# Products of 512 columns that nobody reads in TensorE's waits between an MLP and a state-space block, and one scaling moved behind the second half's addition at the end

## The chip, the cores and the metric

The kernel runs on one core of one Trainium2 chip. The metric is the device time of one execution in microseconds. The kernel before was timed three times: 1705.33, 1705.75 and 1705.82 us, median 1705.75 us.

## The reference

Two transformer-like blocks act in turn on x, 512 tokens by 1024 features, all in float32. Cut to what matters here:

```python
# first block, its end
u2 = rmsnorm(h, norm_mlp_pre)
h = h + rmsnorm(square(relu(u2 @ w_up)) @ w_down, norm_mlp_post)
# second block, its beginning
hn = rms_norm(h, norm_mix_w) * (1.0 + scale) + shift      # scale, shift: from c by adaln
proj = hn @ w_in                                           # convolution, state-space heads, gates
...
# second block, its end
x = x + gate * ((silu(g) * up) @ w_ffn_down)
return rms_norm(x, final_norm_w)
```

So between the MLP and the state-space block stand two norms in a row: that of the MLP's result, and that of the new h. At the end stands one more norm, over the 1024 features of each token.

## The kernel before, in words

Everything is held transposed: 128 partitions by 512 tokens, in 8 chunks of features (`KC = 8`). A weight panel (128 x 2048) comes by DMA from SyncE's queue (`w_raw`, two slots). ScalarE rounds it to `w_hi` (lines 1195 to 1199), GpSimd writes the rest to `w_lo` in four pieces (`low_parts`, line 449). TensorE makes each output tile of 128 x 512 from three products per chunk: high weights by high operand, high weights by low operand, low weights by high operand. Tiles are numbered through the program; tile t goes to the PSUM bank `gemm_bank[t % 4]`. A semaphore `bank_free[b]` counts how often bank b was given back.

The order on each engine is written out by hand, as one program per engine, and the engines wait for each other's semaphores.

**Between MLP and state-space block.** The last tile of the MLP is tile 119, in bank 3; the first tiles of the next block are 120 (`T_DT`, panel 56), 121 and 122 (panel 57), then 123 in bank 3 again. For each token three sums over the features are needed: of the squares of y, of the squares of y times its gain, and of y times gain times h. Seven of eight chunks are added up on VectorE beforehand. TensorE turns these into sums per token by products with a column of ones (`sums_of_parts`, three groups of four; `sums_of_last`, one group of four for `cross`, and one for the last chunk's squares; a float32 product shows as two passes in the profile, so each group is eight records). Then ScalarE takes the root (line 1371), VectorE the reciprocal (line 1711), and TensorE spreads it over the partitions (`spread(3)`, line 562). VectorE scales y (`added_part`, line 2008), GpSimd adds it to h (line 465; on its queue behind the `w_lo` of panel 57), and VectorE scales the new h (`new_operand`, line 2013) by a second spread row, whose root and reciprocal come from a chain of five small steps (`new_step`). ScalarE adds the shift (line 1379), and TensorE begins `first_three` (line 831). In the waits TensorE runs transposes of the identity that nobody reads (`keep_busy`, line 746): 3 ahead of `spread(3)`, 5 behind it, 7 ahead of `first_three`.

VectorE gives bank 3 back (`bank_free[3]`) after it has added tile 119 to y (line 1959); the same addition stands ahead of `cross` (line 1969).

**At the end.** The last tile is made in two halves of 256 tokens. VectorE's order is: addition of half 0 (`last_added(0)`), its reciprocal, five scalings of half 0 (`result(0, range(5))`, line 2441), the addition of half 1 (`last_added(1)`, line 2428), three more scalings of half 0, the reciprocal of half 1 (line 2434), and eight scalings of half 1. Behind the addition of half 1 stand ScalarE's square, TensorE's sums, ScalarE's root, the reciprocal and the spread (line 1161). SyncE's queue sends the results off in nine parts, in order: (0, chunks 0-1), (0, 2-3), (0, 4-5), (0, 6-7), then half 1 by 0-1, 2-3, 4-5, 6, 7, each behind a count of scalings (`out_raw`).

Of the kernel before, what the change touches and what calls it, by code (L numbers as in the profile page):

```python
# [13 lines left out]
P = 128  # L14
S = 512
D = 1024
KC = D // P
# [29 lines left out]
P_DT = P_MLP + MLP_GROUPS * 8  # L47
# [14 lines left out]
T_GRP = T_DT + 1  # L62
# [33 lines left out]
def build(nc, x_in, w_in, cols_in, poolw_in, ada_in, c_in, out):  # L96
# [8 lines left out]
    with ExitStack() as ctx:  # L105
        def sb(name, shape, dt=F32):
            return ctx.enter_context(nc.sbuf_tensor(name, shape, dt))

        def sem(name):
            return ctx.enter_context(nc.semaphore(name))  # L110

        gemm_bank = [ctx.enter_context(nc.psum_tensor(f"gemm_bank{b}", [P, S], F32)) for b in range(4)]
# [3 lines left out]
        whi = [sb(f"w_hi{s}", [P, PANEL], F32R) for s in range(2)]  # L116
# [114 lines left out]
        w_hi_ready = sem("w_hi_ready")  # L231
        w_lo_ready = sem("w_lo_ready")
        tile_done = sem("tile_done")
        bank_free = [sem(f"bank_free{b}") for b in range(4)]
# [128 lines left out]
        def col(name, k):  # L363
            c = COLS[name] + k
            return cols[:, c:c + 1] if isinstance(c, int) else cols[:, bass.ds(c, 1)]
# [114 lines left out]
        def _(pe):  # L480
# [29 lines left out]
            def tile(i, panel, t, p_it, t_it, blocks, hi, lo, ready=None, first=False):  # L510
                tile_high(i, panel, t, p_it, t_it, blocks, hi, lo, ready, first)
                tile_low(i, panel, t, p_it, blocks, hi, first)
# [33 lines left out]
            def wide(j):  # L546

                return [(2 * k + j % 2, k) for k in range(KC)]
# [9 lines left out]
            def spread(n):  # L558

                pe.wait_ge(rinv_ready, n + 1)  # L560
                for j in range(QT):
                    mm = pe.matmul(aux[1][:, j * P:(j + 1) * P], rinv[:, j:j + 1].to_broadcast([P, P]), ident[:, :],
                                   start=True, stop=True)
                mm.then_inc(r_ready, 1)
# [179 lines left out]
            def keep_busy(bank, count):  # L744
                for _ in range(count):
                    pe.transpose(aux[bank][:, P:2 * P], ident[:, :], ident[:, :])
# [21 lines left out]
            def mlp(i, first):  # L768
# [12 lines left out]
                for j in range(2, 8):  # L781
                    tile(i, P_MLP + 4 + j // 2, T_MLP + 8 + j, 8, 16, wide(j), b_hi, b_lo, first=j % 2 == 0)

            def sums_of_parts():

                pe.wait_ge(sq_sum_step, 17)
                pe.wait_ge(gained_step, KC - 2)
                pe.wait_ge(cross_step, 2 * (KC - 2) + 1)
                for n, of in ((0, sq_sum), (1, gained_sum), (2, cross_sum)):
                    for j in range(QT):  # L790
                        mm = pe.matmul(aux[0][:, 3 * j + n:3 * j + n + 1], of[:, j * P:(j + 1) * P], ones[:, 0:1],
                                       start=(n == 0 and j == 0), stop=False, skip_group_check=True)
                mm.then_inc(early_sums, 1)

            def sums_of_last():

                pe.wait_ge(cross_step, 2 * (KC - 2) + 2)
                for j in range(QT):
                    pe.matmul(aux[0][:, 3 * j + 2:3 * j + 3], cross[:, j * P:(j + 1) * P], ones[:, 0:1],
                              start=False, stop=False, skip_group_check=True)  # L800
                pe.wait_ge(ysq_ready, 16)
                for j in range(QT):
                    mm = pe.matmul(aux[0][:, 3 * j:3 * j + 2], sq[:, 1, j * P:(j + 1) * P], one_gain2[:, :],
                                   start=False, stop=(j == QT - 1), skip_group_check=True)
                mm.then_inc(sum_done, 2)

            mlp(0, True)
            with pe.Fori(1, MLP_GROUPS) as i:
                mlp(i, False)
            sums_of_parts()  # L810
            sums_of_last()
            keep_busy(1, 3)
            spread(3)
            keep_busy(2, 5)
            pe.wait_ge(rinv_ready, 5)
            for j in range(QT):
                mm = pe.matmul(aux[2][:, j * P:(j + 1) * P], rinv2[:, j:j + 1].to_broadcast([P, P]), ident[:, :],
                               start=True, stop=True)
            mm.then_inc(r_ready, 1)

            def first_three():

                three = [(P_DT, T_DT, 0), (P_GRP, T_GRP, 0), (P_GRP, T_GRP + 1, 1)]
                for k in range(KC):
                    pe.wait_ge(a_hi_ready, 3 * KC + k + 1)
                    for panel, t, j in three:
                        w = slice((2 * k + j) * P, (2 * k + j + 1) * P)
                        if k == 0:
                            pe.wait_ge(w_hi_ready, panel + 1)
                            pe.wait_ge(bank_free[t % 4], t // 4 + 1)  # L830
                        pe.matmul(gemm_bank[t % 4][:, :], whi[panel % 2][:, w], a_hi[:, k, :], start=(k == 0), stop=False)
                        if k == 0:
                            pe.wait_ge(w_lo_ready, panel + 1)
                        pe.matmul(gemm_bank[t % 4][:, :], wlo[panel % 2][:, w], a_hi[:, k, :], start=False, stop=False)
                for tiles in (three[:1], three[1:]):
                    for k in range(KC):
                        pe.wait_ge(a_lo_ready, 3 * KC + k + 1)
                        for panel, t, j in tiles:
                            w = slice((2 * k + j) * P, (2 * k + j + 1) * P)
                            mm = pe.matmul(gemm_bank[t % 4][:, :], whi[panel % 2][:, w], a_lo[:, k, :],  # L840
                                           start=False, stop=(k == KC - 1))
                            if k == KC - 1:
                                mm.then_inc(tile_done, 1)

            keep_busy(0, 7)
            first_three()
            ident_h = ident[0:SSM_HEADS, 0:SSM_HEADS]

# [182 lines left out]
            for m in range(2):  # L1031
# [6 lines left out]
                if m == 0:  # L1038
                    pe.wait_ge(ginv_ready, 1)
                    for q in (2, 3):  # L1040
                        for j in range(QT):
                            mm = pe.matmul(aux[q][:, j * P:(j + 1) * P],
                                           group_inv[:, 4 * q + j:4 * q + j + 1].to_broadcast([P, P]), ident[:, :],
                                           start=True, stop=True)
# [3 lines left out]
            for q in (0, 1):  # L1048
                for j in range(QT):
                    mm = pe.matmul(aux[q][:, j * P:(j + 1) * P],  # L1050
                                   group_inv[:, 4 * q + j:4 * q + j + 1].to_broadcast([P, P]), ident[:, :],
                                   start=True, stop=True)
# [653 lines left out]
        def _(dve):  # L1706
# [91 lines left out]
            with dve.Fori(0, PAIRS) as i:  # L1798
# [10 lines left out]
                for qt in range(QT + 1):  # L1809
                    if qt < QT:  # L1810
                        n = P * (qt + 1)
# [13 lines left out]
                    if qt >= 1:  # L1825
                        n = P * qt
# [58 lines left out]
            for m in range(KC):  # L1885
                bank = gemm_bank[m % 4][:, :]
# [537 lines left out]
            def last_added(n):  # L2424
                bank = (gemm_bank[(T_END - 1) % 4], aux[3])[n]
                dve.wait_ge(tile_done, T_END + n)
                dve.wait_ge(h_ready, 4 * KC)
                dve.scalar_tensor_tensor(h[:, KC - 1, HALF[n]], bank[:, HALF[n]], mod[:, 24 + 16 + KC - 1:24 + 16 + KC],
                                         h[:, KC - 1, HALF[n]], ALU.mult, ALU.add).then_inc(h_ready, 1)

            def last_inverse(n):
                dve.wait_ge(root_ready, 8 + n)
                dve.wait_ge(rinv_ready, 7 + n)
                dve.reciprocal(rinv[:, 2 * n:2 * n + 2], root[:, 2 * n:2 * n + 2]).then_inc(rinv_ready, 1)

            def result(n, chunks):
                dve.wait_ge(r_ready, 8 + n)
                for k in chunks:
                    if k == KC - 1:
                        dve.wait_ge(h_ready, 5 * KC + n)  # L2440
                    dve.scalar_tensor_tensor(a_raw[:, k, HALF[n]], h[:, k, HALF[n]], col("final_norm_w", k),
                                             aux[1 + n][:, HALF[n]], ALU.mult, ALU.mult).then_inc(out_raw, 1)
# [1 line left out]
            last_added(0)  # L2444
            last_inverse(0)
            dve.wait_ge(h_ready, 5 * KC)
            result(0, range(5))
            last_added(1)
            result(0, range(5, KC))
            last_inverse(1)  # L2450
            result(1, range(KC))

# [97 lines left out]
```

## Time and profile before

| | |
|---|---|
| median of three runs | 1705.75 us |
| the profiled execution, its own time | 1704.91 us |
| its span, from the first to the last instruction | 1703.1 us |
| mean granted TensorE clock | 0.998 |
| TensorE's matmuls busy | 1685.5 us (99%) |
| VectorE, ScalarE, GpSimd busy | 874.3, 704.9, 797.6 us |

The profiled execution's time is 1.8 us more than its span: that lies around the first and last instruction. A row of the timeline gives start and length in us, the engine (PEld is TensorE's weight load, which overlaps its products), the line, output and inputs, and how many instructions were merged; behind it in brackets what ended an idle time. Ends of matmuls are modelled, so their starts are the better measure.

### The profile page before, as it was taken

Reading aid. Unit: us, or ns where it says so; the run is one execution under the profiler, and the core shown is the slowest. Engines: PE = TensorE matmul, PEld = TensorE weight load, DVE = VectorE, ACT = ScalarE, POOL = GpSimd, SP = SyncE. Lnnn points to the kernel's source line nnn. Section 1 sums busy time; section 2 is a strip of 40 time slices with the busy share of each in tenths; the row PEclk is TensorE's granted clock in tenths of the full one; section 3 lists DMA queues with packets and bytes.
Section 4 is the critical chain, followed back from the end, with each engine's and each line's share of the span. In section 5 each row is a group of like instructions: output and inputs, shape, how many; then the busy total and the mean of one; then the engine's idle time right before and its main releaser. Section 6 shows DMA issues by size and latency. Waiting matters only on the chain.

```text
span 1703.1 us, 21894 instructions
## 1 busy us (share of the span) xinstructions
PE 1685.5 (99%) x7971; PEld 1370.9 (80%) x7971; DVE 874.3 (51%) x1361; ACT 704.9 (41%) x975; POOL 797.6 (47%) x608
## 2 busy tenths in 40 slices
PE   9999999899999999999999999999999999999998
PEld 7777777688888888787878888788888888888887
DVE  6234374553616166798897878864445511101113
ACT  5333364431313133457464554784424422222232
POOL 2434344555545454633434434354445544654453
PEclk9999999999999999999999999999999999999999
DMA  5222232265636342233223232322223222332232
GB/s 186 99 74 74 74 111 74 77 224 178 220 117 228 117 173 99 75 125 124 78 99 120 99 123 75 100 98 78 96 83 115 75 99 99 124 127 95 99 124 100
DMA packets 32540, 193.84 MB, mean 114 GB/s; under 512 B 3648, under 2 KB 5696, under 8 KB 13792
## 3 DMA queue, kind: packets, MB, share of 16 engines
q1 hardware_dynamic: 25376, 158.89, 26.7%
q10 hardware_dynamic: 7104, 34.15, 5.7%
q8 instruction: 38, 0.62, 0.1%
q14 instruction: 22, 0.18, 0.0%
HBM read 190.86 MB, written 2.16 MB: 113 GB/s over the span
## 4 chain that ended last, share of the span: by engine, by line
PE 92%; DVE 2%; POOL 2%; issue 2%; DMA 1%; ACT 1%; SPq 0%; DVEq 0%; POOLq 0%
PE gemm_bank L487 24%; PE gemm_bank L494 24%; PE gemm_bank L488 24%; PE gemm_bank L541 4%; PE gemm_bank L525 4%; PE gemm_bank L534 3%; POOL w_lo L449 2%; PE gemm_bank L529 1%; PE aux_bank L915 1%; DMA w_raw<-weights_dram 1%; PE aux_bank L646 1%; PE aux_bank L920 1%; PE aux_bank L900 1%; POOL h L465 1%; PE aux_bank L672 1%
## 5 line engine op out<-in xcount | busy, mean ns | idle before, releaser
L449 POOL TENSOR_TENSOR w_lo<-w_raw,w_hi 128x512 fp32r<-128x512 f32 x580 | 771.1, 1361 | 884.5 <-ACT w_hi L1199 884.5
L487 PE MATMUL gemm_bank<-a_hi,w_hi 128*128 128x512 f32 x1024 | 408.9, 399 | 0.0
L488 PE MATMUL gemm_bank<-a_lo,w_hi 128*128 128x512 f32 x1024 | 399.4, 390 | 0.0
L1199 ACT ACTIVATE w_hi<-w_raw 128x2048 fp32r<-128x2048 f32 x146 | 278.5, 1907 | 184.1 <-PE gemm_bank L494 124.3
L487 PE MATMUL gemm_bank<-b_hi,w_hi 128*128 128x512 f32 x688 | 267.8, 389 | 0.0
L488 PE MATMUL gemm_bank<-b_lo,w_hi 128*128 128x512 f32 x688 | 267.7, 389 | 0.0
L494 PE MATMUL gemm_bank<-a_hi,w_lo 128*128 128x512 f32 x1024 | 258.6, 394 | 0.0
L487 PEld LDWEIGHTS gemm_bank<-a_hi,w_hi 128*128 128x128 f32 x1024 | 192.3, 188 | 44.3 <-issue 5.4
L494 PEld LDWEIGHTS gemm_bank<-a_hi,w_lo 128*128 128x128 f32 x1024 | 190.2, 188 | 44.9 <-issue 6.2
L488 PEld LDWEIGHTS gemm_bank<-a_lo,w_hi 128*128 128x128 f32 x1024 | 192.5, 188 | 40.1 <-issue 1.9
L2098 DVE SCALAR_TENSOR_TENSOR aux_bank<-scratch,gcol,aux_bank 128x511 f32<-128x511 f32 (+15 forms) x240 | 165.8, 734 | 14.2 <-ACT aux_bank L1425 11.9
L494 PE MATMUL gemm_bank<-b_hi,w_lo 128*128 128x512 f32 x688 | 170.6, 389 | 0.0
L488 PEld LDWEIGHTS gemm_bank<-b_lo,w_hi 128*128 128x128 f32 x688 | 129.2, 188 | 26.8
L494 PEld LDWEIGHTS gemm_bank<-b_hi,w_lo 128*128 128x128 f32 x688 | 129.2, 188 | 26.8
L487 PEld LDWEIGHTS gemm_bank<-b_hi,w_hi 128*128 128x128 f32 x688 | 129.1, 188 | 26.8
L2398 DVE TENSOR_TENSOR arena<-arena,gemm_bank 128x512 f32<-128x512 f32 x21 | 14.4, 687 | 174.6 <-PE gemm_bank L494 173.1
L2331 DVE SCALAR_TENSOR_TENSOR h<-gemm_bank,mod,h 128x512 f32<-128x512 f32 x23 | 17.3, 751 | 108.6 <-PE gemm_bank L494 104.9
L487 PE MATMUL gemm_bank<-f_hi,w_hi 128*128 128x512 f32 x165 | 64.2, 389 | 0.0
L488 PE MATMUL gemm_bank<-f_lo,w_hi 128*128 128x512 f32 x165 | 64.2, 389 | 0.0
L1338 ACT ACTIVATE b_hi<-gemm_bank 128x512 fp32r<-128x512 f32 x32 | 19.1, 598 | 107.2 <-DVE gemm_bank L1943 107.2
L1675 ACT ACTIVATE f_hi<-arena 128x512 f32 (+1 forms) x22 | 13.9, 632 | 116.3 <-DVE arena L2398 115.0
L2139 DVE SCALAR_TENSOR_TENSOR sq<-gemm_bank,gcol,sq 128x511 f32<-128x511 f32 (+2 forms) x72 | 53.8, 748 | 13.2 <-ACT sq L1445 11.5
(395 smaller groups left out, 2107.3 us busy)
## 6 DMA issues: line engine op xcount, KB each, us to landing
w_raw<-weights_dram SPq DMA_DIRECT2D x146, 1024.0 KB, 4.7
arena<-ada_dram ACTq DMA_DIRECT2D x32, 768.0 KB, 4.3
acc<-cum_rows ACTq DMA_DIRECT2D x8, 512.0 KB, 3.8
h<-x_t_dram SPq DMA_DIRECT2D x8, 256.0 KB, 6.0
row_b<-cum_rows ACTq DMA_DIRECT2D x4, 512.0 KB, 4.7
scratch<-cum_rows ACTq DMA_DIRECT2D x4, 512.0 KB, 4.3
out_t_dram<-a_raw SPq DMA_DIRECT2D x7, 256.0 KB, 2.2
w_raw<-weights_dram SPq DMA_DIRECT2D x4, 256.0 KB, 5.3
```

Of the source, the lines that this page charges most:

```text
L449: ins = pool.tensor_tensor(wlo[s][:, w], raw[s][:, w], whi[s][:, w].bitcast(F32), ALU.subtract)
L487: pe.matmul(gemm_bank[bank][:, :], whi[slot][:, w], hi[:, k, :], start=(n == 0), stop=False)
L488: pe.matmul(gemm_bank[bank][:, :], whi[slot][:, w], lo[:, k, :], start=False, stop=False)
L494: mm = pe.matmul(gemm_bank[bank][:, :], wlo[slot][:, blk * P:blk * P + P], hi[:, k, :], start=False, stop=(n == last))
L525: pe.matmul(gemm_bank[t % 4][:, :], whi[panel % 2][:, w], hi[:, k, :], start=(n == 0), stop=False)
L534: pe.matmul(gemm_bank[t % 4][:, :], wlo[panel % 2][:, blk * P:blk * P + P], hi[:, k, :], start=False, stop=False)
L541: mm = pe.matmul(gemm_bank[t % 4][:, :], whi[panel % 2][:, blk * P:blk * P + P], lo[:, k, :], start=False, stop=(n == last))
L1199: act.activation(whi[panel % 2][:, :], raw[panel % 2][:, :], ACT.Copy).then_inc(w_hi_ready, 1)
L1338: act.activation(b_hi[:, j, :], bank, ACT.Square).then_inc(b_hi_ready, 1)
L2098: dve.scalar_tensor_tensor(aux[q][:, d:S], u_buf[:, q, 0:S - d], gc(G_CONV_W + CONV_TAPS * q + CONV_TAPS - 1 - d), aux[q][:, d:S], ALU.mul ...
L2139: ins = dve.scalar_tensor_tensor(acc[:, d:S], bank[:, 0:S - d], gc(G_SSM_W + SSM_TAPS * n + SSM_TAPS - 1 - d), acc[:, d:S], ALU.mult, ALU.add)
L2331: dve.scalar_tensor_tensor(hk, gemm_bank[t % 4][:, :], g_, hk, ALU.mult, ALU.add).then_inc(h_ready, 1)
```

## The change

A helper `keep_products` makes products of 128 x 128 by 128 x 512 out of the rounded panel 56 into the bank of tile 123 (bank 3). They take the place of the 3, 5 and 7 transposes (as 3, 4 and 4 products), and four new ones stand among the sums: one behind each of the first two groups of `sums_of_parts`, two between the groups of `sums_of_last`. For this TensorE waits, ahead of `sums_of_parts`, for the rounded panel 56 and for bank 3. At the end, four scalings of half 0 instead of five stand ahead of the addition of half 1, and the one of chunk 7 moves behind the reciprocal of half 1.

```diff
+            MIX_SPARE = (T_GRP + 2) % 4
+
+            def keep_products(bank, count):
+                for _ in range(count):
+                    pe.matmul(bank[:, :], whi[P_DT % 2][:, 0:P], whi[P_DT % 2][:, 0:S], start=True, stop=True)
+
             def sums_of_parts():
 
+                pe.wait_ge(w_hi_ready, P_DT + 1)
+                pe.wait_ge(bank_free[MIX_SPARE], (T_GRP + 2) // 4 + 1)
                 pe.wait_ge(sq_sum_step, 17)
...
                                        start=(n == 0 and j == 0), stop=False, skip_group_check=True)
+                    if n < 2:
+                        keep_products(gemm_bank[MIX_SPARE], 1)
                 mm.then_inc(early_sums, 1)
...
                               start=False, stop=False, skip_group_check=True)
+                keep_products(gemm_bank[MIX_SPARE], 2)
                 pe.wait_ge(ysq_ready, 16)
...
             sums_of_last()
-            keep_busy(1, 3)
+            keep_products(gemm_bank[MIX_SPARE], 3)
             spread(3)
-            keep_busy(2, 5)
+            keep_products(gemm_bank[MIX_SPARE], 4)
             pe.wait_ge(rinv_ready, 5)
...
-            keep_busy(0, 7)
+            keep_products(gemm_bank[MIX_SPARE], 4)
             first_three()
...
             dve.wait_ge(h_ready, 5 * KC)
-            result(0, range(5))
+            result(0, range(4))
             last_added(1)
-            result(0, range(5, KC))
+            result(0, range(4, KC - 1))
             last_inverse(1)
+            result(0, (KC - 1,))
             result(1, range(KC))
```

## Rows read from the trace of the kernel before

**Rows 1.** The page: the chain that ended last, shares of the span by engine.
```profile
PE 92%; DVE 2%; POOL 2%; issue 2%; DMA 1%; ACT 1%; SPq 0%; DVEq 0%; POOLq 0%
```

**Rows 2.** Stretches: us, busy us per engine, the granted clock (PEclk), DMA share, GB/s.
```profile
680.00:681.00 1.00, 1.00 (x11) 1.00 (x10) 0.00 (x0) 0.35 (x1) 0.57 (x1) 1.00 0.01 0
681.00:681.50 0.50, 0.50 (x5) 0.50 (x5) 0.00 (x0) 0.00 (x0) 0.50 (x1) 0.71 0.00 0
...
682.00:682.50 0.50, 0.50 (x4) 0.27 (x3) 0.41 (x3) 0.00 (x0) 0.50 (x1) 0.50 0.00 0
...
684.50:685.00 0.50, 0.50 (x5) 0.35 (x3) 0.50 (x1) 0.00 (x0) 0.50 (x1) 0.88 0.00 0
...
687.00:688.00 1.00, 0.18 (x2) 0.00 (x0) 1.00 (x2) 0.42 (x1) 1.00 (x2) 1.00 0.77 303
```

**Rows 3.** Timeline of TensorE between MLP and state-space block.
```profile
675.18 1.98 PE L494 MATMUL gemm_bank<-b_hi,w_lo 128*128 128x512 f32 x8
...
677.00 0.95 PE L791 MATMUL aux_bank<-ones,dist 128*128 128x1 f32 x8
...
680.49 1.20 PE L803 MATMUL aux_bank<-one_gain,sq 128*128 128x2 f32 x8
...
682.26 2.08 PE L562 MATMUL aux_bank<-ident,rinv 128*128 128x128 f32 x8
...
685.26 1.16 PE L817 MATMUL aux_bank<-ident,rinv 128*128 128x128 f32 x8 [0.18 <-DVE rinv L1711]
...
688.36 0.50 PE L831 MATMUL gemm_bank<-a_hi,w_hi 128*128 128x512 f32 x1 [1.17 <-ACT a_hi L1379]
...
688.69 0.39 PE L834 MATMUL gemm_bank<-a_hi,w_lo 128*128 128x512 f32 x1
...
688.92 0.39 PE L831 MATMUL gemm_bank<-a_hi,w_hi 128*128 128x512 f32 x1
```

**Rows 4.** Timeline of the other engines in the same stretch.
```profile
677.20 0.69 DVE L1959 TENSOR_TENSOR arena<-arena,gemm_bank 128x512 f32<-128x512 f32 x1 [0.62 <-PE gemm_bank L494]
...
678.04 0.75 DVE L1969 SCALAR_TENSOR_TENSOR acc<-arena,cols,h 128x512 f32<-128x512 f32 x1 [0.16 <-DVE arena L1959]
...
680.43 4.94 POOL L449 TENSOR_TENSOR w_lo<-w_raw,w_hi 128x512 fp32r<-128x512 f32 x4 [4.77 <-ACT w_hi L1199]
...
681.73 0.26 ACT L1371 ACTIVATE root<-aux_bank,eps 128x4 f32<-128x4 f32 x1 [1.38 <-PE aux_bank L803]
...
684.37 0.75 DVE L2008 SCALAR_TENSOR_TENSOR tmp<-arena,cols,aux_bank 128x512 f32<-128x512 f32 x1 [1.16 <-PE aux_bank L562]
685.04 0.17 DVE L1711 RECIPROCAL rinv<-root 128x4 f32<-128x4 f32 x1
...
685.32 2.51 POOL L465 TENSOR_TENSOR h<-h,tmp 128x512 f32<-128x512 f32 x2
...
686.74 0.75 DVE L2013 SCALAR_TENSOR_TENSOR a_raw<-h,gain,aux_bank 128x512 f32<-128x512 f32 x1 [0.24 <-POOL h L465]
```

**Rows 5.** Timeline of the end, TensorE and VectorE.
```profile
1692.36 1.47 PE L1148 MATMUL aux_bank<-f_hi,w_lo 128*128 128x256 f32 x11
1692.38 2.05 DVE L2441 SCALAR_TENSOR_TENSOR a_raw<-h,cols,aux_bank 128x256 f32<-128x256 f32 x5 [1.10 <-PE aux_bank L1161]
...
1694.35 0.47 DVE L2428 SCALAR_TENSOR_TENSOR h<-aux_bank,mod,h 128x256 f32<-128x256 f32 x1
1694.75 1.25 DVE L2441 SCALAR_TENSOR_TENSOR a_raw<-h,cols,aux_bank 128x256 f32<-128x256 f32 x3
...
1696.33 0.17 DVE L2434 RECIPROCAL rinv<-root 128x2 f32<-128x2 f32 x1 [0.33 <-ACT root L1701]
...
1697.30 3.22 DVE L2441 SCALAR_TENSOR_TENSOR a_raw<-h,cols,aux_bank 128x256 f32<-128x256 f32 x8 [0.81 <-PE aux_bank L1161]
```

**Rows 6.** Stretches, columns as in the second group: the other norm's waits, and the end.
```profile
312.00:315.00 3.00, 2.24 (x14) 1.70 (x12) 0.69 (x1) 1.08 (x2) 0.00 (x0) 1.00 0.63 183
...
1698.00:1699.00 1.00, 0.00 (x0) 0.00 (x0) 1.00 (x4) 0.00 (x0) 0.00 (x0) 0.69 0.00 0
```

## The prediction

> **What bounds the kernel now.** I began with the chain that ended last: TensorE holds 92% of it [rows 1], so a change is worth what it does where TensorE does not multiply. The diff touches two such places. Then I cut the first place into short stretches. The reader should see that the granted clock is 1.00 up to 681.0 us, falls at about 681.2 (the stretch of 681.0 to 681.5 shows 0.71), stays at 0.50 and is back at about 684.6 [rows 2]: about 3.4 us at the lower of the two levels, 1.2 instead of 2.4 GHz. Ahead of the fall TensorE had run, from 677.00 to 681.3, nothing but five groups of products one or two columns wide [rows 3]. In the other norm's wait, with transposes around a single such group, the stretch from 312 to 315 keeps 1.00 [rows 6]. Third, the timeline of this place, to find who is waited for. The MLP's last products start at 675.18, the sums at 677.00, the last group at 680.49, ScalarE's root at 681.73, the first spread at 682.26 [rows 3, 4]. The spread takes 2.08 us, and the like spread at 685.26, with the clock back, 1.16 us [rows 3]: 0.92 us is what the fall costs on the path. Then VectorE scales from 684.37, GpSimd adds from 685.32, VectorE makes the operand from 686.74, and the first product comes at 688.36 [rows 3, 4]. Note how near GpSimd's queue is: its last `w_lo` ends at 680.43 + 4.94 = 685.37, the first scaling at 684.37 + 0.75 = 685.12 [rows 4]. So an earlier first scaling could give nothing at all; GpSimd would still begin at 685.37. In 687 to 688 TensorE has 0.18 us of work and yet the clock is 1.00 [rows 2]. Last, the end: a serial chain through VectorE [rows 5].
>
> **The change part by part.**
>
> *The wait for bank 3.* VectorE gives it back behind the addition of tile 119, which ends at 677.20 + 0.69 = 677.89, and ahead of `cross`, which starts at 678.04 [rows 4]. The sums now start at about 678.07 instead of 677.00 [rows 3]: 1.07 us late (0.95 to 1.1). The early sums were made just while VectorE added the last tile; the wait uncovers them. Behind the waiting instruction are all five groups, so all of it goes on. ScalarE has room: its squares and the rounding of panel 57 do not wait for these sums. The wait for the rounded panel 56 costs nothing; its `w_lo` is made from it, and GpSimd is past that and waits for panel 57 until 680.43 [rows 4].
>
> *Four products among the sums.* The path runs through them: they stand on TensorE's own queue ahead of the last group. Their price is not shown, so I bound it by products of 512 columns: 0.33 us from start to start for one whose neighbour began after a pause, 0.23 in a stream [rows 3]. Two stand alone between groups and two in a pair: 3 x 0.33 + 0.23 = 1.22 us; in a pure stream 4 x 0.23 = 0.92; if each change between narrow and wide products costs another 0.1, about 1.6. I take 1.22, as they stand mostly alone. A gain from them by themselves is excluded, since they are extra instructions in order.
>
> *The last group.* Starts of the groups are (680.49 - 677.00) / 4 = 0.87 us apart, and from the start of the last to the root are 1.24 us, of which some 0.15 lie in the fallen clock [rows 3, 4]. If the clock stays up, that is given back.
>
> The root therefore moves by 1.07 + 1.22 - 0.15 = 2.14 us, from 681.73 to 683.87.
>
> *The clock.* If the four products keep it at 1.00, the first spread costs 1.16 instead of 2.08: -0.92. The first scaling then starts 2.14 - 0.92 = 1.22 late, at 685.59, and ends at 686.34. GpSimd is then no longer held by `w_lo` but by this: it starts at about 686.37 instead of 685.32, 1.05 late. The 0.25 us by which it had been held by its own queue is the cover that is used up.
>
> *3, 4 and 4 products instead of 3, 5 and 7 transposes.* The three end at about root time + 0.6 while the reciprocal comes at root + 0.5: at most 0.1. The four (0.92 to 1.02 us) stand in the wait for the second reciprocal, which follows the first scaling on VectorE (685.04 behind 684.37 [rows 4]) and has 1 us of room; the last four stand in the wait of TensorE from 686.4 to 688.36 [rows 3]. Both nothing; without that cover they would cost a product each, 0.23.
>
> *The second spread.* From its reciprocal at 685.04 to the end of the spread (685.26 + 1.16 = 686.42) are 1.38 us [rows 3, 4]. Now the reciprocal comes at 685.59 + 0.67 = 686.26 and the spread ends at 687.64. GpSimd's first addition ends at 686.37 + 1.29 = 687.66, and VectorE is free of three scalings at 687.72. The operand starts at 687.76 instead of 686.74: 1.02 late. Behind it the pace is as before (one addition on GpSimd per 1.26 us, six products of 0.23 on TensorE), so the whole program behind it is 1.0 us late. `w_lo` of panel 57 and the panels' DMAs stand ahead of the additions in their queues and don't move; later panels move with the tiles.
>
> *The end.* Five scalings stand ahead of the second addition, from 692.38 to 694.35: 0.39 us each. TensorE's last products end at 692.36 + 1.47 = 693.83 [rows 5]. With four, VectorE is free at 693.96, so the addition comes 0.39 us sooner, and still VectorE, not TensorE, sets it. Square, sums, root follow it. Three scalings end at about 695.6, the root at 695.9, so the reciprocal is not held back; it was at 696.33 and comes at 695.94. The scaling moved behind it costs 0.39 to 0.45, in the wait for the spread, which was 0.81 us [rows 5]. On SyncE's queue the part with chunks 6 and 7 of half 0 goes off about 0.5 us later, at 696.6, and holds no later part, the next being ready at 697.7. So the last eight scalings start at 696.91 instead of 697.30: -0.39 us.
>
> **Sum.** Against the profiled execution, 1704.91 us (span 1703.1 plus 1.8 around it): +1.0 - 0.4 = 1705.5. That execution lies 0.84 below the median of the runs, 1705.75; against the median it is 1706.35, and I write 1706.3.
>
> **A rule against the rows.** The clock came back at 684.6 after a stretch that held eight transposes and the spread's eight passes, with no product 512 wide [rows 2, 3]. The Trainium skill ("TensorE: Matmul & The Clock Gate", section "Part 4: PE-mode transpose") says that transposes do not count as busy in the way products do; by it the replaced ones would be worth something. By the rows the clock is back from 684.6 on, over most of the 5 and all of the 7 transposes, so this sum stays at +0.6 by either. Where the rule bears is on the rival with a lasting fall: real products in later waits make it less likely, and I leave it only a few in a hundred.
>
> **The rivals.**
>
> *The clock falls all the same.* Two products among three narrow groups may not do what a stream does: the clock also falls at 1698.4, behind the end's transposes, sums and spread [rows 5, 6]. Then the last 16 passes run at half speed: a group that takes 0.87 took 1.24 or more, at full length twice 0.87, so 2 x 0.87 more, and nothing of the 0.15 is kept; the pair costs 0.5 more, less what falls behind the return of the clock (about 0.7). The root comes 1.6 later than in my sum, with the spread at full clock again: +0.6 + 1.6 = +2.2, 1707.9. For it: the same kind of work made the fall before. 0.24.
>
> *The delay is hidden.* If the products cost nothing next to the sums' weight loads, the first scaling is 1.07 - 0.15 - 0.92 = 0.0 late and only the end's gain is left: -0.4, 1705.35. Against: these loads are already back to back, as the busy weight load shows (1.00 of 1.00 in 680 to 681 [rows 2]). 0.12.
>
> *Slower by over 0.2%: the fall lasts into the operand's wait.* Place: the three products, the first spread and the four products. The case above, and the clock then stays at 0.50 through the first spread: the three products end 0.7 later than the reciprocal, and the spread costs 0.92 more. +2.2 + 0.7 + 0.9 = +3.8, 1709.5. It decides from the point where the first spread shows 2.08 us again. Against: it came back with transposes alone. 0.04.
>
> *The end's step gives nothing,* because the last scalings are held by something other than their spread: then +1.0, 1706.75; it lies in my range. Part of the 0.58 of the forecast.
>
> **How the numbers follow.** Forecast 0.58, fallen clock 0.24, hidden 0.12, lasting fall 0.04, and 0.02 for what I don't see. The forecast's own width: the products from 0.92 to 1.6 and the wait from 0.95 make it -0.4 to +0.5, and the runs spread by 0.5. The range takes in the hidden case and the fallen clock: 1705.0 to 1708.2. A measurement of this kernel can tell about 0.2%, here 3.4 us: only the lasting fall reaches it. Faster by that much would need more than all the waits of both places that the change can touch (the 0.92 and the 0.39): 0.01. Slower 0.05, within 0.94.
>
> **What would show it.** Right: the first group of sums begins behind the addition of tile 119; it and the last group are about 4.7 us apart instead of 3.5; root at 683.9 on the old scale; first spread near 1.16 us; first product near 689.4; in the end 1.6 us from the first scaling to the second addition instead of 1.97. Wrong: a first spread of about 2 us or a clock of 0.50 in the sums (the fallen clock), GpSimd's first addition still at 685.4 (hidden), a clock below 1.00 past 686.

## The result, and the profile after

The changed kernel is slower: median 1708.88 us (20 runs, 1707.87 to 1711.17) against 1705.38 us (20 runs of the kernel before beside them, 1704.66 to 1707.85), ratio 1.0018 with a 95% interval of 1.0012 to 1.0024. That is 3.5 us by the medians, where +0.6 was forecast and 1708.2 was the upper end of the range. The profiled execution took 1708.65 us, span 1706.9: 3.7 us more than that of before. In the experiments one further run of the kernel before, of 9704 us, is left out.

The granted clock in the place between MLP and state-space block, by the stretches of the changed kernel (columns as in [rows 2]):

```profile
680.00:681.00 1.00, 1.00 (x10) 0.96 (x9) 0.00 (x0) 0.55 (x1) 0.37 (x1) 1.00 0.12 49
681.00:682.00 1.00, 1.00 (x10) 1.00 (x9) 0.00 (x0) 0.00 (x0) 1.00 (x2) 0.85 0.00 0
682.00:683.00 1.00, 1.00 (x6) 1.00 (x6) 0.00 (x0) 0.00 (x0) 1.00 (x1) 0.50 0.00 0
...
687.00:688.00 1.00, 1.00 (x6) 1.00 (x6) 0.01 (x1) 0.26 (x1) 0.00 (x0) 0.50 0.79 262
688.00:689.00 1.00, 1.00 (x7) 0.91 (x6) 0.29 (x1) 0.00 (x0) 0.00 (x0) 0.73 1.06 442
```

The clock falls at about 681.7 and is back at about 688.5: 6.8 us at the lower level instead of 3.4 [rows 2]. So the four products among the sums did not keep it up. The reader should also see that TensorE is busy 1.00 of 1.00 in each of these stretches: a share of busy time tells nothing of this. The timeline of TensorE and of those it works for, in the changed kernel:

```profile
677.40 0.69 DVE L1970 TENSOR_TENSOR arena<-arena,gemm_bank 128x512 f32<-128x512 f32 x1 [0.61 <-PE gemm_bank L494]
...
678.25 1.02 PE L799 MATMUL aux_bank<-ones,dist 128*128 128x1 f32 x8 [0.88 <-issue]
...
679.13 0.48 PE L788 MATMUL gemm_bank<-w_hi 128*128 128x512 f32 x1
...
679.44 0.95 PE L799 MATMUL aux_bank<-ones,acc 128*128 128x1 f32 x8
...
681.38 1.55 PE L809 MATMUL aux_bank<-ones,acc 128*128 128x1 f32 x8
...
682.78 1.20 PE L788 MATMUL gemm_bank<-w_hi 128*128 128x512 f32 x2
...
683.78 1.70 PE L814 MATMUL aux_bank<-one_gain,sq 128*128 128x2 f32 x8
...
685.34 1.63 PE L788 MATMUL gemm_bank<-w_hi 128*128 128x512 f32 x3
685.52 0.26 ACT L1382 ACTIVATE root<-aux_bank,eps 128x4 f32<-128x4 f32 x1 [4.97 <-PE aux_bank L814]
...
685.82 0.18 DVE L1722 RECIPROCAL rinv<-root 128x4 f32<-128x4 f32 x1 [6.81 <-ACT root L1382]
...
686.77 1.90 PE L562 MATMUL aux_bank<-ident,rinv 128*128 128x128 f32 x8
...
688.71 0.75 DVE L2019 SCALAR_TENSOR_TENSOR tmp<-arena,cols,aux_bank 128x512 f32<-128x512 f32 x1 [1.70 <-PE aux_bank L562]
...
689.54 2.51 POOL L465 TENSOR_TENSOR h<-h,tmp 128x512 f32<-128x512 f32 x2 [3.96 <-DVE tmp L2019]
...
692.55 0.49 PE L842 MATMUL gemm_bank<-a_hi,w_hi 128*128 128x512 f32 x1 [0.86 <-ACT a_hi L1390]
```

I count from the start of VectorE's addition of tile 119: 677.20 before [rows 4], 677.40 here. The sums start 0.85 behind it instead of 0.20 ahead of it: 1.05 late, as forecast. A product alone between groups costs 679.44 - 679.13 = 0.31 us, as taken. But from the start of the group at 681.38 to the root are 4.14 us, where full clock would give about 0.87 + 0.56 + 1.1 = 2.5 (a group, 0.87 [rows 3]; two products, 0.31 + 0.25; and 1.07 from the last group's start to the root, as in e1 below). The other 1.6 us are the low clock on the path. The root comes at +8.12 (before +4.53), the first scaling at +11.31 (before +7.17), the first product at +15.15 (before +11.16): 4.0 us late. With the addition itself 0.2 later than before and the end's -0.4, that makes up the 3.8 us by which the span grew. GpSimd, which in the kernel before began right behind its own `w_lo` [rows 4], now idles 3.96 us for the first scaling.

The end, VectorE's timeline in the changed kernel:

```profile
1696.59 1.66 DVE L2452 SCALAR_TENSOR_TENSOR a_raw<-h,cols,aux_bank 128x256 f32<-128x256 f32 x4 [1.10 <-PE aux_bank L1172]
...
1698.16 0.48 DVE L2439 SCALAR_TENSOR_TENSOR h<-aux_bank,mod,h 128x256 f32<-128x256 f32 x1
...
1700.15 0.17 DVE L2445 RECIPROCAL rinv<-root 128x2 f32<-128x2 f32 x1 [0.33 <-ACT root L1712]
1700.23 0.48 DVE L2452 SCALAR_TENSOR_TENSOR a_raw<-h,cols,aux_bank 128x256 f32<-128x256 f32 x1
...
1701.12 3.22 DVE L2452 SCALAR_TENSOR_TENSOR a_raw<-h,cols,aux_bank 128x256 f32<-128x256 f32 x8 [0.41 <-PE aux_bank L1172]
```

From the first scaling to the last eight are 4.53 us, before 4.92 [rows 5]: -0.39, as worked out. The moved scaling stands in the spread's wait, which shrinks from 0.81 to 0.41.

### The profile page after: what moved, and what is told of

Its sections match the earlier page's. It is cut to its first block, busy times and chain, and to the rows that moved or that the text cites. A ratio compares the mean times of both kernels' runs of the same rounds, so it can differ in the third digit from the quotient of the medians.

```text
span 1706.9 us, 21896 instructions
## 1 busy us (share of the span) xinstructions
PE 1689.1 (99%) x7971; PEld 1373.7 (80%) x7971; DVE 874.4 (51%) x1361; ACT 705.1 (41%) x975; POOL 797.6 (47%) x608
## 4 chain that ended last, share of the span: by engine, by line
PE 95%; DVE 2%; POOL 1%; DMA 1%; ACT 0%; SPq 0%; issue 0%; DVEq 0%; POOLq 0%
PE gemm_bank L487 25%; PE gemm_bank L494 25%; PE gemm_bank L488 25%; PE gemm_bank L541 4%; PE gemm_bank L525 4%; PE gemm_bank L534 3%; PE gemm_bank L529 1%; PE aux_bank L926 1%; PE aux_bank L646 1%; PE aux_bank L931 1%; PE aux_bank L911 1%; POOL h L465 1%; PE aux_bank L672 1%; PE aux_bank L663 1%; DMA w_raw<-weights_dram 1%; PE aux_bank L904 0%
```

## The experiments

Two theories stood at first. A: the low clock on the path is what costs, and whatever makes the path late lets more of it run at that clock. B: TensorE's pause ahead of the sums keeps the clock low. The rival to both was that the products' and the wait's own time is all there is. The kernels ran in four groups (e1 to e4, e5 to e8, e9 and e10, e11 and e12), each group beside runs of the kernel before; the difference given is that of the medians, against the runs of its own group. The intervals are about 0.0009 to each side, 1.5 us, so the smaller differences do not stand clear of them, and each reading leans on a trace too. A trace is of one execution, and "+8.12" always means 8.12 us behind the start of the addition of tile 119 in it.

That start itself lay between 677.20 and 679.07 us in the fourteen profiles. In ten of them, all but those of the kernel before, the changed kernel, e9 and e11, the clock had already been low for 3.4 us, once or twice, between 317 and 340 us, in the first block, where all these kernels have the same code. Twice was in e2, e5 and e6, and there the addition came 1.1 to 1.9 us later than in the kernel before. So part of the spread of each kernel's times has nothing to do with the place that the change touches.

**e1, the end alone.**

```diff
-            result(0, range(5))
+            result(0, range(4))
             last_added(1)
-            result(0, range(5, KC))
+            result(0, range(4, KC - 1))
             last_inverse(1)
+            result(0, (KC - 1,))
```

> Only the end's step of the change; everything up to there as before. Both theories of the stage between MLP and state-space block expect nothing there (root 4.53 us behind VectorE's addition of tile 119, as before). If the step is worth what it showed in the changed kernel's trace, the last eight scalings start 0.39 us sooner and the time is 0.4 us below before, too small for the interval; if the addition of the second half were held by TensorE instead, 0.1 us or nothing.

Measured 1705.31 us, -0.37 (ratio 0.9998, 0.9989 to 1.0007): no difference by the interval. Its trace shows the last eight scalings 4.53 us behind the first (1693.63 to 1698.16), as in the changed kernel. It also shows something of the stage, where its code is that of before: the clock fell 1.2 us later behind the addition of tile 119 than in the profile of the kernel before, so that the last group ran at full speed and the first scaling came at +6.70 instead of +7.17. GpSimd still began at +8.14 (+8.12 before), and the first product at +11.16 both times. The earlier scaling gave nothing, since GpSimd was busy with `w_lo` until then (681.66 + 4.95 = 686.61, and it began at 686.57).

**e2, the wait alone.**

```diff
             def sums_of_parts():
 
+                pe.wait_ge(w_hi_ready, P_DT + 1)
+                pe.wait_ge(bank_free[(T_GRP + 2) % 4], (T_GRP + 2) // 4 + 1)
                 pe.wait_ge(sq_sum_step, 17)
```

> The kernel before plus the two waits ahead of the sums, no products, transposes kept, end as before. Theory A (the low clock lasting over two spans is what costs, and the products among the sums, slow at that clock, drag it on): one low span of 3.4 us that ends before or in the first spread, root 1.1 us later than before (5.6 us behind the addition of tile 119), time +0.8 to +1.1 us. Theory B (the pause of TensorE ahead of the sums is what keeps the clock low): clock at 0.50 past the first spread, time +2 us or more.

Measured 1707.11 us, +1.4 (ratio 1.0009, 1.0000 to 1.0018), but from 1705.83 to 1710.07. The profiled execution was the slowest of them, with 10.2 us at the low level. Its stretches and its groups of sums:

```profile
680.00:681.00 1.00, 1.00 (x11) 1.00 (x11) 0.54 (x1) 1.00 (x2) 0.00 (x0) 1.00 1.09 459
681.00:682.00 1.00, 1.00 (x8) 1.00 (x7) 0.00 (x0) 1.00 (x1) 0.00 (x0) 0.61 0.57 238
...
690.00:691.00 1.00, 1.00 (x6) 0.74 (x5) 1.00 (x3) 0.00 (x0) 0.34 (x1) 0.50 0.93 393
691.00:692.00 1.00, 1.00 (x8) 1.00 (x9) 0.96 (x2) 0.00 (x0) 1.00 (x2) 0.77 0.41 156
```

```profile
679.79 1.02 PE L793 MATMUL aux_bank<-ones,dist 128*128 128x1 f32 x8 [0.89 <-issue]
680.68 1.36 PE L793 MATMUL aux_bank<-ones,acc 128*128 128x1 f32 x8
681.90 1.84 PE L793 MATMUL aux_bank<-ones,row_b 128*128 128x1 f32 x8
683.60 1.84 PE L801 MATMUL aux_bank<-ones,acc 128*128 128x1 f32 x8
```

A group of sums takes 683.60 - 681.90 = 1.70 us at the lower level instead of 0.89. With the clock down during three groups the root came at +8.24, as late as in the changed kernel, without one added instruction, and the first product at +14.98. So in this execution, where the clock fell early (+2.3), the wait cost 3.8 us in the stage; its other lateness, 1.75 us, stood ahead of the stage. By the median the cost is nearer to A's +0.8 to +1.1, and the profile shows the long low time of B: this run does not decide. That the wait costs only its own 1 us where the clock stays up is seen in e11 against e9; no trace shows a fast execution of e2.

**e3, products among the sums, but no wait.** The changed kernel with tile 122's bank, free long before:

```diff
-            MIX_SPARE = (T_GRP + 2) % 4
+            MIX_SPARE = (T_GRP + 1) % 4
...
-                pe.wait_ge(bank_free[MIX_SPARE], (T_GRP + 2) // 4 + 1)
+                pe.wait_ge(bank_free[MIX_SPARE], (T_GRP + 1) // 4 + 1)
```

> The changed kernel with the spare products written to the bank of tile 122, free much sooner, so that the sums need not wait for the addition of tile 119; all else as changed. Theory A (products among the sums at the low clock drag it on, wherever the sums begin): still about 6.8 us at 0.50, the cost of the stage falls only by the wait's 1.05, time +2.5 us against before. Theory B (the pause does it): clock holds or is low for one span only, time between -0.4 and +1.0 us.

Measured 1707.22 us, +1.5 (ratio 1.0008, 0.9999 to 1.0017). Its stretches, addition and first product:

```profile
682.00:683.00 1.00, 1.00 (x4) 0.81 (x4) 0.00 (x0) 0.00 (x0) 1.00 (x2) 0.50 0.00 0
...
687.00:688.00 1.00, 1.00 (x6) 0.90 (x6) 0.23 (x1) 0.00 (x0) 0.00 (x0) 0.50 0.78 147
```

```profile
677.92 0.69 DVE L1970 TENSOR_TENSOR arena<-arena,gemm_bank 128x512 f32<-128x512 f32 x1 [0.62 <-PE gemm_bank L494]
...
691.62 0.50 PE L842 MATMUL gemm_bank<-a_hi,w_hi 128*128 128x512 f32 x1 [0.81 <-ACT a_hi L1390]
```

TensorE had no pause ahead of the sums, and still 6.8 us were low, first product at +13.70. So a pause is not needed for the long low time; B as the only cause falls. The expected +2.5 was too high.

**e4, products only behind the sums** (the four among the sums taken out, the wait moved behind `sums_of_last`).

```diff
             sums_of_last()
+            pe.wait_ge(w_hi_ready, P_DT + 1)
+            pe.wait_ge(bank_free[MIX_SPARE], (T_GRP + 2) // 4 + 1)
             keep_products(gemm_bank[MIX_SPARE], 3)
```

> The changed kernel without the four products among the sums and with the wait behind the sums; the 3, 4 and 4 products stand in place of the 3, 5 and 7 transposes, the end as changed. Theory A: the sums run as before, the clock falls in the last group as before, but three products of 512 at the low clock take about 1.3 us in place of the transposes' 0.7, so the first spread is about 0.5 us later, one low span, and with the end's -0.4 the time is 0 to +0.3. If the products in the waits bring the clock back sooner than transposes do, the first spread is 1.2 us and the time -0.6.

Measured 1705.13 us, -0.55 (ratio 1.0000, 0.9991 to 1.0009): what the end gives, within the noise. One low time of 3.4 us, first product at +11.18. Both expectations rested on a fall in the last group; here, as in e1, the clock fell only in the first spread (+5.3). So the three products ran at full clock, and with that the 3, 4 and 4 products cost and gave nothing in place of 3, 5 and 7 transposes. What the three cost at the low clock e6 shows.

**e5, twice the products, no wait** (e3 with two, two and four).

```diff
                     if n < 2:
-                        keep_products(gemm_bank[MIX_SPARE], 1)
+                        keep_products(gemm_bank[MIX_SPARE], 2)
...
-                keep_products(gemm_bank[MIX_SPARE], 2)
+                keep_products(gemm_bank[MIX_SPARE], 4)
```

> As the changed kernel with the spare products in the bank of tile 122 (no wait for tile 119's addition), but two, two and four products among the sums instead of one, one and two. If more products hold the clock: 1.00 through the sums and the first spread, the four added ones cost 4 x 0.23 = 0.92 us on the path, and the time lies about 0.3 us below that of the one with one, one and two, near +1.2 against before. If they don't: the added ones at the low clock cost up to 2 x 0.92, time +2.8 or more.

Measured 1708.84 us, +3.3 (ratio 1.0016, 1.0007 to 1.0025). The clock fell, later (at about 683.9, +5.6), and the low time again was 6.8 us, now reaching into the second spread. Behind this fall only the rest of the last group stood ahead of the three products and the spread. The first product came at +14.59:

```profile
678.31 0.69 DVE L1970 TENSOR_TENSOR arena<-arena,gemm_bank 128x512 f32<-128x512 f32 x1 [0.62 <-PE gemm_bank L494]
...
692.90 0.50 PE L842 MATMUL gemm_bank<-a_hi,w_hi 128*128 128x512 f32 x1 [0.79 <-ACT a_hi L1390]
```

**e6, the wait and the products behind, none among the sums** (the changed kernel without the four).

```diff
-                    if n < 2:
-                        keep_products(gemm_bank[MIX_SPARE], 1)
...
-                keep_products(gemm_bank[MIX_SPARE], 2)
                 pe.wait_ge(ysq_ready, 16)
```

> The changed kernel (wait ahead of the sums, 3, 4 and 4 products in the waits behind them, end as changed) without the four products among the sums. The wait alone gave +1.4 by medians and the end -0.4, so +1.0 if the parts add up, and the four products are then worth the other 2.5 us of the change. If wait and products cost more together than apart (because both push the path into a second low span), more than +1.5.

Measured 1707.94 us, +2.4 (ratio 1.0014, 1.0005 to 1.0023). With e4's -0.55 and e2's +1.4 the parts would add up to about +0.9. The measured +2.4 is 1.5 more, about the width of one interval, so the medians alone do not show that wait and wide products cost more together. The profiles show part of it. This one (again the slowest of its runs, 10.2 us low, fall at +2.2) is alike with e2's up to the root (+8.29, e2 +8.24). Then the three products run in the low clock, 1.4 us from the first to the spread's start, where e2's three transposes had made way after 0.7, and the first product comes at +15.51, 0.5 us behind e2's +14.98.

**e7, transposes for the products among the sums** (two for each, the changed kernel otherwise).

```diff
+            def spare_turns(count):
+                for _ in range(count):
+                    pe.transpose(gemm_bank[MIX_SPARE][:, 0:P], ident[:, :], ident[:, :])
...
-                        keep_products(gemm_bank[MIX_SPARE], 1)
+                        spare_turns(2)
...
-                keep_products(gemm_bank[MIX_SPARE], 2)
+                spare_turns(4)
```

**e8, the stage alone** (the changed kernel with the end of before).

```diff
-            result(0, range(4))
+            result(0, range(5))
             last_added(1)
-            result(0, range(4, KC - 1))
+            result(0, range(5, KC))
             last_inverse(1)
-            result(0, (KC - 1,))
```

> The changed kernel without the end's step. The stage alone: 0.4 us above the changed kernel, +3.9 against before; the trace of the end as before (1.97 us from the first scaling to the second addition).

Measured 1709.52 us, +4.0 (ratio 1.0025, 1.0016 to 1.0034), where +3.9 was expected. The end in its trace is that of before: 1697.07 to 1699.04, 1.97 us. In the stage, whose code is that of the changed kernel, 10.2 us were low instead of 6.8, and the first product came at +16.40 instead of +15.15.

**e9 and e12, four and three products behind each of the first four groups, no wait.** This is the deciding pair for the clock as a cost of its own: many more instructions on the path. Both use tile 122's bank as e3 does; e12 has 3 in both places where e9 has 4.

```diff
                         mm = pe.matmul(aux[0][:, 3 * j + n:3 * j + n + 1], of[:, j * P:(j + 1) * P], ones[:, 0:1],
                                        start=(n == 0 and j == 0), stop=False, skip_group_check=True)
-                    if n < 2:
-                        keep_products(gemm_bank[MIX_SPARE], 1)
+                    keep_products(gemm_bank[MIX_SPARE], 4)
...
-                keep_products(gemm_bank[MIX_SPARE], 2)
+                keep_products(gemm_bank[MIX_SPARE], 4)
```

> As the doubled one (bank of tile 122, no wait), but four products behind each of the first four groups of sums, 16 in all. If the low clock is a cost of its own that a stream of products can prevent: clock at 1.00 through sums and both spreads, root 16 x 0.23 + 0.3 - 0.1, about 3.9 us later than before, first spread 1.2 us instead of 2.1, first scaling 2.9 later, GpSimd 2.7 later, and with the end's -0.4 a time of +2.3: below the doubled one (+3.3) with eight products more. If the low clock is no cost of its own, or products don't hold it: +5 us or more.

> As the one with four each and no wait, but three behind each of the first four groups. If three still hold the clock: 4 x 0.23 = 0.9 less, +0.7. If they don't in every execution: a wide spread of times and a median above +1.6, up to the +3.3 of the doubled one.

e9 measured 1707.07 us, +1.6 (ratio 1.0008, 0.9999 to 1.0017), e12 1706.70 us, +1.1 (1.0004, 0.9995 to 1.0013). The time of e9 was expected at +2.3, that of e12 at +0.7. Stretches of e12's profile, where e3 shows 0.50:

```profile
682.00:683.00 1.00, 1.00 (x10) 0.95 (x9) 0.00 (x0) 0.00 (x0) 1.00 (x2) 1.00 0.00 0
...
687.00:688.00 1.00, 1.00 (x7) 0.62 (x6) 1.00 (x4) 0.00 (x0) 0.68 (x1) 1.00 0.69 115
```

And its timeline at the addition, the root, the first spread and the first product:

```profile
677.62 0.69 DVE L1969 TENSOR_TENSOR arena<-arena,gemm_bank 128x512 f32<-128x512 f32 x1 [0.63 <-PE gemm_bank L494]
...
684.76 0.26 ACT L1381 ACTIVATE root<-aux_bank,eps 128x4 f32<-128x4 f32 x1 [3.99 <-PE aux_bank L813]
...
685.37 1.08 PE L562 MATMUL aux_bank<-ident,rinv 128*128 128x128 f32 x8
...
686.49 0.75 DVE L2018 SCALAR_TENSOR_TENSOR tmp<-arena,cols,aux_bank 128x512 f32<-128x512 f32 x1 [0.24 <-PE aux_bank L562]
...
690.34 0.50 PE L841 MATMUL gemm_bank<-a_hi,w_hi 128*128 128x512 f32 x1 [0.88 <-ACT a_hi L1389]
```

Twelve products among the sums, and the first product comes at +12.72; with four (e3) it came at +13.70. Eight more instructions of 0.24 us on the path, and 1 us sooner: the low clock is a cost of its own, and the few products bought none of it back. The spread takes 1.08 us instead of 1.91. The times say the same most clearly against e5: e12 has four products more on the path and e9 eight, yet both were faster by 2.1 and 1.8 us, and ten of e5's eleven runs (1708.34 us and more) lie above every run of e9 and e12 (up to 1707.70). This rules out the rival that the added instructions' own time is all there is.

The runs of e12 lie within 1705.95 to 1707.11, while 21 of the 107 runs of the kernel before in these studies lie above 1706.7, up to 1708.3, all with a mean clock of 0.995 or less. As many of its runs below 1706.7 have such a clock too, and no trace shows in which place the clock was low in them.

**e10, the wait without the pause** (e2 with four products into tile 122's bank ahead of the wait for bank 3).

```diff
+                pe.wait_ge(bank_free[(T_GRP + 1) % 4], (T_GRP + 1) // 4 + 1)
+                keep_products(gemm_bank[(T_GRP + 1) % 4], 4)
                 pe.wait_ge(bank_free[(T_GRP + 2) % 4], (T_GRP + 2) // 4 + 1)
```

> The kernel before plus the wait for bank 3 ahead of the sums, but with four products (0.9 us, bank of tile 122) run ahead of that wait, so that TensorE is late by the same 1.05 us and yet not idle; transposes and end as before. If the idle pause of 0.9 us itself brings the longer low time: one low span, +0.9 us. If it is the lateness alone (the last group and the spread pushed further into the low clock, wherever it falls), the same as the wait alone by median, +1.4.

Measured 1707.03 us, +1.6 (ratio 1.0006, 0.9997 to 1.0015), the same by median as the wait alone (+1.4). In its profile the clock was low for 6.8 us, from +3.95 on, with no pause and no product between the groups, and the first product came at +13.34:

```profile
682.50:683.00 0.50, 0.50 (x4) 0.50 (x4) 0.00 (x0) 0.00 (x0) 0.50 (x1) 0.50 0.00 0
...
687.50:688.00 0.50, 0.50 (x4) 0.24 (x2) 0.50 (x3) 0.00 (x0) 0.23 (x1) 0.50 0.46 197
```

So by the median the lateness costs it, not the pause, and late sums alone can come with the long low time. All runs of e10 lie between 1706.46 and 1707.42, where e2 had three above 1708.5. Whether the pause made those is not shown: the one that was profiled lost 1.75 us ahead of this place.

**e11, four products each, with the wait** (e9 with bank 3).

> The changed kernel with four products behind each of the first four groups of sums instead of one, one, none and two (bank of tile 123, so the wait for tile 119's addition stands). Without the wait the same 16 products held the clock and gave +1.6. If they hold it here too, the wait costs its 1.05 us and nothing else: +2.6, and the changed kernel with twelve products more is faster than the changed kernel (+3.5). If the pause of 0.9 us lets the clock fall all the same, +5 or more.

Measured 1708.95 us, +3.4 (ratio 1.0021, 1.0012 to 1.0030); +2.6 was expected. In its profile the clock held, and there the wait costs just its time: root at +9.19 (e9 +8.08), first product at +14.77 (e9 +13.65), 1.1 us each. The first product comes 0.4 us sooner than in the changed kernel (+15.15), with twelve products more on the path. But that execution was the fastest of its kernel, at 1708.13 us, with a mean clock of 0.999. One more had 0.999, at 1708.15; the other nine had 0.994 to 0.998 and took 1708.53 to 1714.09 us. The two are near where the expectation put them (+2.5). Whether the clock fell in the others behind the pause no trace shows, and the 0.8 us by the median stay open.

No kernel is shown faster than the kernel before. e1 and e4 lie 0.4 and 0.55 us below it, within their intervals.

## Why the prediction was wrong

*Where it failed* is the step called "The clock": "If the four products keep it at 1.00". They did not; the clock fell as before and stayed down twice as long. The forecast rested on this with 0.58, and the case that came was the last but one of the rivals, "the fall lasts into the operand's wait", with 0.04. Its price, worked out as +3.8, is near what the medians gave (+3.5), by the mechanism named. The last groups were slow: +1.6, as the first rival has it, and as measured (4.14 - 2.5). The three products ran past the reciprocal: 686.77 - 685.82 = 0.95 us from the reciprocal's start to the spread, before 0.23, from 682.03 to 682.26 [rows 3]; the sum of this rival has 0.7 more, and 0.72 came. The spread took 1.90 us, 0.74 more than at full clock. So the mechanism stood there, and the chance was wrong. That the median came so near is in part luck, since the same code had 6.8 us low in one profile and 10.2 in another (e8). The row from the trace of before that this rests on:

```profile
682.03 0.18 DVE L1711 RECIPROCAL rinv<-root 128x4 f32<-128x4 f32 x1 [3.23 <-ACT root L1371]
```

*Why the chance was wrong.* I argued "Against: it came back with transposes alone". That was read from a kernel in which, behind the fall, only the last group was left, and then the spread and transposes followed. In the changed kernel the sums start 1.05 us later and are drawn out, so that behind the fall stood most of a group, two products, and another group: mostly the same kind of work that had stood ahead of the fall. The rows for that were there [rows 3]: the first rival let these groups run slowly, and yet had the clock back for the spread. That it was this work that kept the clock down is argued, not shown. It fits e2, e3, e7 and e10, where one group or more still stood behind the fall; but in e5 only the rest of one did, and the low time was as long.

A second ground was weaker than it looked. I read from the other norm's wait that transposes around a single group of sums keep the clock up [rows 6], but that stretch ends at 315 us, where this group begins (314.95). In that trace the clock did stay at 1.00 behind it too. But in the profiles of e4, e7 and e12, with the same code there, the clock fell in the spread behind it, at 317.4 to 317.8 us (granted clock 0.50 in 318 to 319). Also, the 0.5 us by which I let the runs spread came from three runs; the twenty that were compared spread by 3.2 us.

*What held.* The wait, 1.05 us. The four products were priced a little too high, at 1.22. From start to start a single one costs 0.31, but the group behind it then makes way after 0.81 instead of 0.89: the last group starts 2.87 us later with twelve products (e12) and 3.80 with sixteen (e9), 0.24 each, so 0.96 for four. At a held clock the rest of the sum holds: e11's root at +9.19, less twelve products of 0.24 that the change does not have, is +6.3, and I had 683.87 - 677.20 = +6.67; of the 0.4 between, 0.26 is the products' price. The products behind the sums are worth nothing where the clock is up as the first three run (e4), and cost 0.5 us where it is low (e6 against e2). The 0.25 us of cover by GpSimd was real, and it holds the other way too: e1's first scaling 0.47 sooner moved nothing, as the prediction had said it could. The end's 0.39 came out to the hundredth in the traces (in the medians, -0.37, it is inside the noise). "Slower by over 0.2%" needed 3.4 us. By the medians 3.5 came; the ratio, 1.0018 (1.0012 to 1.0024), leaves open on which side of 0.2% it lies.

*The rule against the rows.* That transposes do not count as busy in the way products do (the Trainium skill, "TensorE: Matmul & The Clock Gate", "Part 4: PE-mode transpose") had lowered my chance for the lasting fall. The runs show no difference between the two here: e4 replaced fifteen transposes by eleven products at one low time of 3.4 us as before, and e7 with transposes was as fast as the changed kernel with products. That does not test the rule in a place where it would decide, but here it should have moved no chance.

*How the parts make the whole.* By medians: the end -0.4 (e1), the wait +1.4 (e2), the products among the sums about +1.9 without the wait (e3 against the end alone), which with the end makes +2.9; together they gave +3.5. The 0.6 between is smaller than the intervals and is not explained. Of these the low clock's share cannot be given to the tenth, since it differs from execution to execution.

## What to carry to other kernels

Filler among instructions that are themselves the path costs its own time (0.24 us a product here), and if it is too little to hold the clock it costs twice, as TensorE's work behind the fall then runs slower (e3 and e5). Enough of it held the clock (e9, e12) and was still not faster than the kernel before. Before adding a buffer's wait ahead of such a sequence, look for one whose last reader is long done (tile 122's bank here), and look at what the engine will be doing after the fall, not only ahead of it. And a place where the clock falls must be judged over many executions, since the moment of the fall is not the same in each, and a single slow profile can have lost its time elsewhere (e2).

## What the runs showed of the hardware

The moment of the fall moves with respect to the program: with the same code in the stage it came 4.0 us (the first profile) and 5.2 us (e1) behind the start of the addition of tile 119. In the fourteen profiles the low time in this place was 3.4, 6.8 or 10.2 us, or none (e9, e11, e12). It was 3.4 only in the kernel before, e1 and e4, where the sums start ahead of the addition and have nothing between them. Ahead of the fall TensorE was not idle: its matmuls and weight loads were busy 1.00 of 1.00 from 680 to 681 us [rows 2]. A group of eight one-column passes takes 0.89 us at the higher level and 1.70 at the lower. In e2 the eight weight loads of such a group take 0.97 and 1.83 us, about the whole of it, and so they slow down with the clock.
